# A two-tile expert search: more dot products inside the search, and sixty dense chunks ahead of the slot transposes

## What is computed

```python
q = (xc @ w_query).reshape(C, PEER_HEADS, 2, PEER_HALF)
sc = jnp.einsum('thpd,hpnd->thpn', q, sub_keys)
top_s, top_i = lax.top_k(sc, PEER_TOPK)
...
best_s, best_pos = lax.top_k(cand_s, PEER_TOPK)
experts = jnp.take_along_axis(cand_i, best_pos, axis=-1)
gates = jax.nn.softmax(best_s, axis=-1)
u = expert_down[experts]
vv = expert_up[experts]
act = jax.nn.gelu(jnp.einsum('cd,chkd->chk', xc, u), approximate=False)
return jnp.einsum('chk,chkd->cd', gates * act, vv)
```

## Time and profile before

| | |
|---|---|
| median of 3 runs | 1423.78 us (1422.45 to 1424.66) |
| the profiled execution: time, span | 1425.13 us, 1423.3 us |
| TensorE, VectorE, ScalarE, GpSimd busy | 89%, 61%, 31%, 21% of the span |
| read from HBM | 371.84 MB |
| the expert layer | about 183 to 890 us of the span |

### The profile page before, as it was taken

The page is one execution under the profiler, slowest core; times in us unless marked ns, Lnnn a source line. Parts: engine busy times, 40 slices in busy tenths (PEclk is TensorE's granted clock), DMA queues, the critical chain, the costliest instruction groups (busy, mean ns, idle before and its releaser), DMA issues. The chain is left out here.

```text
span 1423.3 us, 20146 instructions
## 1 busy us (share of the span) xinstructions
PE 1271.9 (89%) x6925; PEld 973.1 (68%) x6925; DVE 862.7 (61%) x2026; ACT 443.8 (31%) x1019; POOL 292.7 (21%) x270
## 2 busy tenths in 40 slices
PE   7998999996999887777777778999999999989998
PEld 4665489995998775222222222899999998569994
DVE  5567557999998556445554444555565553357761
ACT  2443212002981000000000000465666554246651
POOL 0000001554677344333333330000000000000000
PEclk9999999999999999999999999999999999999999
DMA  8340079899999999999999998855455462065520
GB/s 319 119 170 1 1 277 377 304 380 409 365 409 409 409 409 409 409 409 410 409 410 409 410 409 344 265 175 165 155 160 156 130 200 80 25 190 171 141 91 30
DMA packets 163961, 374.31 MB, mean 263 GB/s; under 512 B 42016, under 2 KB 91680, under 8 KB 162336
## 3 DMA queue, kind: packets, MB, share of 16 engines
q1 hardware_dynamic: 127008, 238.93, 46.9%
q0 software_dynamic: 36864, 134.23, 24.0%
HBM read 371.84 MB, written 1.29 MB: 262 GB/s over the span
## 5 line engine op out<-in xcount | busy, mean ns | idle before, releaser
L1526 PE MATMUL select_four<-ring,table 128*128 128x512 f32 x512 | 255.6, 624 | 75.9 <-DMA ring<-in_up 75.9
L1777 DVE SCALAR_TENSOR_TENSOR x<-table,select_act_u,x 128x1024 f32<-128x1024 f32 x128 | 164.4, 1284 | 160.6 <-DMA table<-in_up,select_expert 160.3
L1526 PEld LDWEIGHTS select_four<-ring,table 128*128 128x128 f32 x512 | 88.2, 191 | 242.6 <-DMA ring<-in_up 172.9
L1460 POOL DMA_INDIRECT table<-in_down_rows,select_expert x128 | 162.4, 1269 | 352.3 <-DVE select_expert L1650 218.8
L1336 PE MATMUL plain_u<-whole,ring 128*128 128x128 f32 x1696 | 207.8, 279 | 28.5 <-DMA ring<-in_downT 27.2
L1336 PEld LDWEIGHTS plain_u<-whole,ring 128*128 128x128 f32 x1696 | 195.4, 192 | 39.6 <-DMA ring<-in_downT 38.2
L1657 DVE CUSTOM_DVE_ANT_0 table<-table,h_row 128x1024 f32<-128x1024 f32 x128 | 152.6, 1222 | 52.8 <-DMA table<-in_down_rows,select_expert 51.6
L1460 POOL DMA_INDIRECT table<-in_up,select_expert x128 | 123.6, 966 | 201.2 <-DVE x L1777 180.0
L245 PE MATMUL mix_a_pj<-mix_a_wh,hT_high 128*128 128x384 f32 x368 | 129.1, 351 | 0.0
L247 PE MATMUL mix_a_pj<-mix_a_wh,hT_low 128*128 128x384 f32 x368 | 123.5, 336 | 0.0
L246 PE MATMUL mix_a_pj<-mix_a_wl,hT_high 128*128 128x384 f32 x368 | 123.4, 335 | 0.0
(11 more groups left out here) (376 smaller groups left out, 2108.4 us busy)
## 6 DMA issues: line engine op xcount, KB each, us to landing
ring<-in_up SPq DMA_DIRECT2D x128, 512.0 KB
ring<-in_downT SPq DMA_DIRECT2D x106, 512.0 KB
mix_raw<-in_wa SPq DMA_DIRECT2D x46, 768.0 KB, 6.1
block_w_raw<-in_w SPq DMA_DIRECT2D x16, 768.0 KB, 6.4
mix_raw<-in_wb SPq DMA_DIRECT2D x16, 768.0 KB, 7.2
ring<-in_route SPq DMA_DIRECT2D x16, 576.0 KB, 6.2
table<-in_downT SPq DMA_DIRECT2D x18, 512.0 KB, 6.7
wo<-in_wo SPq DMA_DIRECT2D x4, 1024.0 KB, 8.4
```

The source lines that it names most:

```text
L1460: pool.indirect_dma_start(gathered[s % GATHERS], None, rows, bass.IndirectOffsetOnAxis(ap=expert[:, s % SLOTS:s % SLOTS + 1], axis=0)).the ...
L1526: mm = pe.matmul(four[:, h, :], table[:, 1, n, :], up_rows[n % RING][:, h * 512:(h + 1) * 512], start=n == 0, stop=n == NKEYS - 1)
L1777: dve.scalar_tensor_tensor(x[:, 0, :], gathered[b], act_u[:, s:s + 1], x[:, 0, :], ALU.mult, ALU.add).then_inc(dotted, 1)
```

## The change

Two lines of constants. `DOTS_FIRST` goes from 2 to 4 and `DOTS_LISTS` from 2 to 3: the dots that VectorE does within the two searches go up by 3 x 2 + 4 x 1 = 10, and those left for the last joins go down from 48 to 38. `AHEAD` goes from 52 to 60: TensorE does eight more dense chunks before the four transposes and eight fewer between the groups.

```diff
-AHEAD = 52
+AHEAD = 60
 BESIDE = 32
 WAITING = BESIDE // 4
-DOTS_FIRST, DOTS_LISTS, DOTS_PAIRS, DOTS_INDEX, DOTS_TURN = 2, 2, 3, 5, 3
+DOTS_FIRST, DOTS_LISTS, DOTS_PAIRS, DOTS_INDEX, DOTS_TURN = 4, 3, 3, 5, 3
```

## The result

The changed kernel took 1433.66 us (1430.58 to 1434.34, 4 runs) against 1424.22 us before in the same comparison: a ratio of 1.0062 (95% interval 1.005 to 1.0075). A second comparison gave 1431.02 against 1423.12 us, 1.0052 (1.0038 to 1.0066). The forecast had the sign and the places; 1427 us was too little, and its range ended at 1433. By the first ratio the change costs 8.8 us, nearly three times the forecast's 3.1. The profiled execution is the fastest of the four, 1430.58 us with a span of 1428.8 us, 5.5 us over the span before. A second profile has a span of 1428.6 us.

What follows compares the result with a forecast made beforehand. The prediction took the two DMA queues as the bound: the stage's time is its transfers, dry time and TensorE's remaining work. Terms -2.6 + 0 + 1.7 + 4.0 = +3.1 us gave about 1427 us, range 1420 to 1433.

Steps and rivals of the forecast that it cites:

- Step (2): Transposes behind eight more chunks: slot copy moves from 352.65 to about 373 us, VectorE and ScalarE waiting for TensorE.
- step (3): Chunk 56 needs the GELU of PSUM group 12, delayed behind VectorE's scores; it just fits: 0 us.
- Step (4): Handover from the chunks to the groups: much the same hole in the queues, 0 us, between -2 and +4.
- Step (5): The 16 groups: fewer chunks asked for in each, so queues run a little dry: +1.7 us, lower bound 0.
- Step (6): Gathers lead dense rows by 9 more, leaving rows for TensorE at the stage's end: +4.0 us, bounds 0 and 5.3.
- step (1): Early dots free gather buffers, so more gathers land between 252 and 294 us: -2.6 us, bounds 0 and -7.7.
- The tail: Dense rows left to TensorE when gathers are through, at the stage's end: +4.0 us for 9 rows.
- B: Rival: faster, six early gathers land in dry time and extra chunks close the 360 to 380 us hole; 1418 us, chance 0.17.
- C: Rival: no change, small lead as joins and the `up` pause level the streams; 1424.4 us, chance 0.21.
- D: Rival: clearly slower, GpSimd can't issue gathers while VectorE runs the early dots; +10.7 us, 1434.5 us, chance 0.12.

Runs made afterwards that it cites:

- gap filled: Kernel before, with three of the 28 chunks between groups moved behind the transposes, ahead of the first group: 1419.79 us, 0.9973.
- chunks alone: Kernel before with AHEAD 60 in place of 52, dots as before: 1431.49 us, 1.0058.
- dots alone: Kernel before with the ten dots moved forward, 52 chunks ahead: 1431.5 us, 1.0057.
- sixty, dots later: Changed kernel with its six dots of the first tile's lists moved behind the index searches, sixty chunks ahead: 1425.56 us, 1.0017 against the kernel before.
- gap, dots early: Kernel before with the changed kernel's ten dots forward, 52 chunks ahead and three in the gap behind the transposes: 1427.85 us, 1.0033.
- gap, dots later: Kernel before with three chunks in the gap and ten dots forward, behind the index searches and in the second tile's lists: 1423.34 us, 1.0006.

## Why the prediction was right in kind and short in size

**What held.** The bound is the two queues. The gap filled with three chunks took off 3.8 us with the same work for every engine and the copy at the same time. And the profiles agree on it. Dry us are (409 - rate) x width / 409 for the windows 252 to 294, 360 to 410 (the hole at the handover), 410 to 460 (the groups) and 560 to 580 us (from `down` to `up`). The three rows from "gap filled" on have 52 chunks ahead; the stage's end is the start of the next layer's first matmuls:

| | copy | 252-294 | hole | groups | to `up` | dry, sum | stage's end | end - dry |
|---|---|---|---|---|---|---|---|---|
| before | 352.65 | 11.7 | 3.9 | 0 | 0 | 15.6 | 890.1 | 874.4 |
| changed | 374.54 | 11.3 | 3.9 | 2.0 | 2.0 | 19.1 | 895.5 | 876.3 |
| changed, 2nd profile | 374.45 | 9.1 | 6.3 | 3.2 | 2.9 | 21.6 | 897.4 | 875.8 |
| chunks alone | 365.78 | 10.8 | 8.8 | 1.8 | 0 | 21.4 | 896.4 | 875.0 |
| dots alone | 368.82 | 9.0 | 10.0 | 0 | 3.6 | 22.6 | 898.4 | 875.7 |
| sixty, dots later | 371.82 | 11.2 | 1.2 | 2.2 | 2.7 | 17.4 | 894.4 | 877.0 |
| gap filled | 352.65 | 10.7 | 1.5 | 0 | 0 | 12.2 | 886.4 | 874.2 |
| gap, dots early | 368.38 | 9.3 | 5.6 | 0 | 4.0 | 18.9 | 895.0 | 876.1 |
| gap, dots later | 364.14 | 10.7 | 0.2 | 0.1 | 2.7 | 13.7 | 888.9 | 875.2 |

The end moves over 12 us, the end without the dry time over 3, and it is least where the lead is small. The copy's lateness doesn't order the runs: the chunks alone end later than the sixty with the dots later, with the copy 6 us earlier.

Step (2): the copy was predicted at 373 and came at 374.5, with VectorE waiting for TensorE; step (3): no wait for the GELU. Step (4): a hole much like the old one, 3.9 us for 3.9, in the first profile; 6.3 in the second. The windows of the changed kernel that part the hole from the groups:

```profile
380.00:410.00 30.00, 25.36 (x206) 24.78 (x205) 27.01 (x45) 28.29 (x70) 19.74 (x14) 0.94 0.96 356
410.00:460.00 50.00, 44.19 (x382) 43.14 (x383) 48.58 (x78) 35.99 (x84) 36.88 (x27) 1.00 1.01 393
```

And in its second profile, with the change from `down` to `up`:

```profile
380.00:410.00 30.00, 26.06 (x204) 25.68 (x202) 26.68 (x45) 27.87 (x68) 19.42 (x14) 0.89 0.91 323
410.00:460.00 50.00, 44.18 (x370) 43.32 (x371) 47.62 (x76) 35.94 (x85) 36.16 (x26) 0.97 1.00 383
...
560.00:580.00 20.00, 14.65 (x99) 12.18 (x100) 10.94 (x16) 1.50 (x3) 10.19 (x9) 0.94 0.95 349
```

Step (5) had the groups at +1.7 us; they measured +2.0 and +3.2. Step (6): the lead is there. At 600 us VectorE has begun 18 updates and TensorE done 10 rows, at 870 us 124 and 115; before it was 17 and 14, 122 and 119. The Trainium skill ("DMA: Bandwidth & Descriptors", SWDGE vs HWDGE vs iDMA) has each DMA engine go round-robin between the two kinds of queue, and the trace agrees: the lead stays at 8 to 9 rows for 270 us.

**What failed: step (1).** I put "-2.6 us" for early gathers and only 11.5 us for VectorE's lateness. I asked what a dot frees and not what it needs. The first gathers land 2.56 us apart (the dots at 243.16, 245.72, 248.28), while a dot takes 1.15 us. So the third and fourth dot stood and waited, the scores came 15.4 us late, and the pause of GpSimd was only shifted. The first profile shows no gain (299 for 295 GB/s, 0.3 pieces), the second the 2.0 pieces that I had taken, but with more missing later. At the later places the six dots cost 5.0 us less with sixty chunks, 3.8 us less with the gap filled, and nearly all of it shows in the hole at the handover (3.9 and 6.3 us against 1.2; 5.6 against 0.2).

**What the sum had at nothing: the change from `down` to `up`.** The prediction took the queues as full from 450 us on. In every profile with all ten dots moved, and in none without, they run dry by 2.0 to 4.0 us between 555 and 580 us. In the changed kernel GpSimd waits there 3.54 us, to 575.37, for the first update of `x` to free a buffer. That this is the whole cause isn't shown.

**The sum.** Dry time was to change by -2.6 + 0 + 1.7 = -0.9 us. It changed by -0.4 + 0 + 2.0 + 2.0 = +3.6 in the first profile and by -2.6 + 2.4 + 3.2 + 2.9 = +5.9 in the second. The tail was to cost +4.0 for nine more rows of lead; six more came, 2.6 us by the same price, and what the dry time leaves of the stage's +5.4 and +7.3 us is 1.8 and 1.4. So the forecast's dry time was 4.5 to 6.8 us too low and its tail 2 to 3 us too high.

**From profile to median.** The two profiled executions took 5.5 and 5.3 us more than the one before, the medians are 9.4 and 7.9 us apart. The difference is where the profiled ones lie: the one before was 0.9 and 2.0 us above the two medians before, those of the changed kernel 3.1 and 0.6 us below theirs. What its slower executions lose no profile shows.

**Rivals.** B (faster) failed: the early gathers brought 0.3 pieces in one profile and 2.0 in the other, for B's six, and the pause of VectorE for TensorE came true. C (streams that end level) failed by the lead. D named the right amount of harm for another reason: GpSimd's issues were not much longer (165.8 us for 128 against 162.4), so its trap is not what happened.

**Open.** Why dots placed early at 250 us show up as a wider hole at the handover, and not where they wait: the window of 252 to 294 us is no better with the dots later (300 and 305 GB/s, for 299 to 320 with them early). The runs show that it does, in two pairs, and not by which requests. Nor is it shown why the hole is 9 to 10 us with the chunks or the dots alone and 4 to 6 with both. Moving gathers to a third queue wasn't tried.

## What to carry to other kernels

When transfers set the time, count the requests: an edit gains only if it puts a request into a stretch in which a queue is dry, and an engine's gap is best filled with work that frees a buffer. Before work is moved forward to free a buffer sooner, look when its own data lands: a consumer ahead of its producer holds up everything behind it. Of two chains that meet, making one longer alone cost 8 us here, and making both longer, with the dots at the later places, 2.4: judge such a change by the dry time of every stretch behind it, and not by how late the meeting is.

## What was not expected of the hardware

A lead of one stream over the other, once there, stayed at 8 to 9 rows from 600 to 870 us, with both at one piece in 2.56 us, and ten dense rows were then multiplied without a wait at the end. And the same program is more or less dry in the same window from one execution to the next: for the changed kernel 379 and 360 GB/s between 380 and 460 us, as here in its first profile:

```profile
380.00:460.00 80.00, 69.55 (x588) 67.92 (x588) 75.58 (x122) 64.29 (x153) 56.62 (x40) 0.98 0.99 379
```
